# Hybrid RG-LRU / retention / expert-choice MoE step on one core: the recurrence's gates moved one chunk earlier, its chain cut by direction, and the final norm done tile by tile

## What is computed

```python
h = rms_norm(x) * (1 + sc1) + sh1                   # sc, sh, g: from ada_w and the condition
xl, yl, q, k, v, g = split(h @ w_in)                # six blocks of 512 columns
xl = depthwise_conv4(xl)
r, gi = sigmoid(xl @ wa[d] + ba[d]), sigmoid(xl @ wi[d] + bi[d])      # d = forward, backward
log_a = -8 * r * softplus(-lam);  a = exp(log_a)
u = sqrt(-expm1(2 * log_a)) * gi * xl
h_t = a_t * h_(t-1) + u_t                           # scanned in both directions, then summed
lru_out = (hf + hb) * gelu(yl)
ret_out = rms(retention(rope(q), rope(k), v)) * silu(g)
x1 = x + g1 * rms_norm(concat(lru_out, ret_out) @ w_out)
h2 = rms_norm(x1) * (1 + sc2) + sh2
f = 16 experts, each takes its top tokens (64 latent, 16 context): silu(h2 wg) * (h2 wu) @ wd, added up
y = x1 + g2 * rms_norm(f)
```

## Time and profile before

| | us |
|---|---|
| median of 3 runs | 1654.58 (1652.83 to 1656.48) |
| the profiled execution, its own time | 1652.98 |
| its span, first to last instruction | 1651.2 |
| PE busy | 1516.5 (92% of the span) |
| DVE busy | 1282.8 (78%) |
| ACT busy | 1008.4 (61%) |
| POOL busy | 194.0 (12%) |
| mean granted clock of PE, of 1 | 0.949 |

### The profile page before, as it was taken

The page is one execution under the profiler, slowest core; times in us unless marked ns, Lnnn a source line. Parts: engine busy times, 40 slices in busy tenths (PEclk is TensorE's granted clock), DMA queues, the critical chain, the costliest instruction groups (busy, mean ns, idle before and its releaser), DMA issues.

```text
span 1651.2 us, 19540 instructions
## 1 busy us (share of the span) xinstructions
PE 1516.5 (92%) x7022; PEld 1052.7 (64%) x7022; DVE 1282.8 (78%) x1127; ACT 1008.4 (61%) x807; POOL 194.0 (12%) x110
## 2 busy tenths in 40 slices
PE   5799898879948999999999999999999999999991
PEld 2698776547745666666666666666666666666650
DVE  5647736784557988989889898898988989889873
ACT  6313444242325777777777777777777777777752
POOL 0301210000000020220202202022020220201200
PEclk9899899999858999999999999999999999999995
DMA  9421123357138999999999999999999999999943
GB/s 354 125 77 52 51 77 97 100 199 296 41 101 307 364 371 379 390 359 381 376 375 376 364 384 372 373 387 359 385 373 367 386 366 382 369 375 369 367 186 135
DMA packets 127667, 476.71 MB, mean 289 GB/s; under 512 B 11406, under 2 KB 21898, under 8 KB 111244
## 3 DMA queue, kind: packets, MB, share of 16 engines
q1 hardware_dynamic: 116304, 447.77, 72.7%
q0 software_dynamic: 3728, 13.11, 3.1%
q10 hardware_dynamic: 7596, 15.30, 2.6%
HBM read 462.51 MB, written 13.64 MB: 288 GB/s over the span
## 4 chain that ended last, share of the span: by engine, by line
PE 83%; DVE 8%; ACT 3%; DMA 3%; issue 2%; POOL 0%; SPq 0%; ACTq 0%; POOLq 0%; DVEq 0%
PE banks L965 22%; PE banks L969 22%; PE banks L966 22%; PE banks L329 3%; PE banks L330 3%; PE banks L331 3%; PE banks L986 2%; DVE w_lo L295 1%; ACT w_hi L291 1%; DMA raw<-in_ada_w 1%; PE banks L919 1%; PE banks L758 1%; PE banks L836 1%; PE banks L955 1%; DVE arena L1184 1%
## 5 line engine op out<-in xcount | busy, mean ns | idle before, releaser
L295 DVE TENSOR_TENSOR w_lo<-raw,w_hi 128x2048 fp32r<-128x2048 f32 x232 | 531.1, 2290 | 174.0 <-ACT w_hi L291 169.7
L291 ACT CAST w_hi<-raw 128x2048 fp32r<-128x2048 f32 x232 | 443.1, 1912 | 134.7 <-PE banks L969 66.5
L965 PE MATMUL banks<-w_hi,act_lo 128*80 128x512 f32 x1152 | 457.5, 397 | 1.7 <-DVE act_lo L1414 1.7
L966 PE MATMUL banks<-w_hi,act_hi 128*80 128x512 f32 x1152 | 454.9, 395 | 0.0
L969 PE MATMUL banks<-w_lo,act_hi 128*80 128x512 f32 x1152 | 314.6, 395 | 0.0
L295 DVE TENSOR_TENSOR w_lo<-arena,w_hi 128x2048 fp32r<-128x2048 f32 x96 | 220.0, 2291 | 37.7 <-ACT w_hi L291 37.7
L965 PEld LDWEIGHTS banks<-w_hi,act_lo 128*80 128x80 f32 x1152 | 173.2, 150 | 95.6 <-issue 2.6
L969 PEld LDWEIGHTS banks<-w_lo,act_hi 128*80 128x80 f32 x1152 | 171.0, 148 | 96.7 <-issue 1.4
L966 PEld LDWEIGHTS banks<-w_hi,act_hi 128*80 128x80 f32 x1152 | 171.7, 149 | 92.4 <-issue 1.6
L291 ACT CAST w_hi<-arena 128x2048 fp32r<-128x2048 f32 x96 | 183.6, 1913 | 62.4 <-PE banks L969 62.4
L295 DVE TENSOR_TENSOR act_lo<-raw,act_hi 128x2048 fp32r<-128x2048 f32 x64 | 146.7, 2292 | 17.3 <-ACT act_hi L291 17.3
(11 more groups left out here) (225 smaller groups left out, 1764.7 us busy)
## 6 DMA issues: line engine op xcount, KB each, us to landing
raw<-in_exp_down SPq DMA_DIRECT2D x126, 1024.0 KB, 7.0
raw<-in_exp_gate SPq DMA_DIRECT2D x66, 1024.0 KB, 7.6
arena<-in_exp_up SPq DMA_DIRECT2D x64, 1024.0 KB, 7.6
raw<-in_exp_up SPq DMA_DIRECT2D x64, 1024.0 KB, 8.0
arena<-in_exp_gate SPq DMA_DIRECT2D x62, 1024.0 KB, 7.4
raw<-in_ada_w SPq DMA_DIRECT2D x24, 1024.0 KB, 5.6
raw<-in_w_in SPq DMA_DIRECT2D x12, 1024.0 KB, 5.2
arena<-in_x_lat ACTq DMA_DIRECT2D x8, 512.0 KB, 10.4
```

The lines of the kernel that those rows point to most:

```text
L291: nc.scalar.copy(w_chunk(w_hi, n), raw_chunk(n)).then_inc(hi_done, 1)
L295: nc.vector.tensor_tensor(w_chunk(w_lo, n), raw_chunk(n), w_chunk(w_hi, n), ALU.subtract).then_inc(lo_done, 1)
L965: mm(dst, x[j][1], wh[:, j, at], start=(first and j == 0), stop=False)
L966: mm(dst, x[j][0], wh[:, j, at], start=False, stop=False)
```

## The change

Four edits. (1) Chunk `ct` of the recurrence moves from the first half of block `2 + ct` to the second half of block `1 + ct`. In blocks xl, q and k its four PE steps stand inside and behind the last unit (after k = 1, 3, 5 and 7); in block v behind tiles 0 to 3 of the second half. ACT does all of the chunk, exp, tanh and roots too, before it splits the next weight chunk; in block v it copies tiles of v between the gates. DVE's parts move to the first half of the next block, and the `split_lo` of the half before stands behind `lru_scan`. (2) POOL's product, DVE's square, weighting and product, and ACT's root are cut by direction, each with its own count. (3) ACT issues the retention loads of heads 0 and 1 before the second last split of block g, not after g's tiles. (4) At the end POOL copies the last column of indices before it waits for expert 15's rows; ACT takes a root ahead, which loads that table early; DVE multiplies each tile with the gain before its root is known, and then does one fused operation; squares, roots and sums run tile by tile; SP issues the stores.

```diff
-GATES_AT = {0: 0, 2: 1, 4: 2, 6: 3}
+    g_times = raw[:, 0:3, :].rearrange("p r (t d) -> p (r t) d", t=2)
...
 # SP, behind the loads of the five tiles
+        for t in range(TILES):
+            sync.wait_ge(fin_y, t + 1)
+            sync.dma_start(y_lat[t * P:(t + 1) * P, :] if t < 4 else y_ctx, facc[:, t, :]).then_inc(out_y, 16)
...
 # ACT
         def lru_sqrt(ct):
-            act.wait_ge(lr_w, ct + 1)
-            nc.scalar.activation(lr_t[:, :, :], lr_t[:, :, :], ACT.Sqrt).then_inc(lr_sq, 1)
+            for d in range(2):
+                act.wait_ge(lr_w, 2 * ct + d + 1)
+                nc.scalar.activation(lr_t[:, d, :], lr_t[:, d, :], ACT.Sqrt).then_inc(lr_sq, 1)
...
         for m in range(N_WIN, N_MID):
             bi, half = (m - N_WIN) // 2, m % 2
-            ct = GATES_AT.get(m - N_WIN - 4)
+            ct = bi - 1 if half and 1 <= bi <= CT else None
             if ct is not None:
-                for s in range(4 * ct, 4 * ct + 4):
-                    lru_gates_out(s)
-
+                for j in range(4):
+                    lru_gates_out(4 * ct + j)
+                    if bi == 4:
+                        tok_out(0, j)
+                if bi == 4:
+                    tok_out(0, TILES - 1)
+                lru_exp(ct)
+                lru_sqrt(ct)
             if bi == 0:
                 yl_out(2 * half)
-            if half and bi >= 4:
-                for t in range(TILES - 1):
-                    tok_out(bi - 4, t)
             if half and bi == 5:
-                tok_out(1, TILES - 1)
+                for t in range(TILES):
+                    tok_out(1, t)
+            if bi == 5 and not half:
                 ret_loads(0)
                 ret_loads(1)
             split_hi(act, m + WS)
...
-            if half and bi == 4:
-                tok_out(0, TILES - 1)
-            if ct is not None:
-                lru_exp(ct)
-                lru_sqrt(ct)
...
-        for t in range(TILES):
-            act.wait_ge(f_in[t], 16)
+        nc.scalar.activation(sm[:, S_X1:S_X1 + 8], sm[:, S_X1:S_X1 + 8], ACT.Sqrt).then_inc(root_warm, 1)
+        for t in range(TILES + 1):
+            if t < TILES:
+                act.wait_ge(f_in[t], 16)
+                if t == 0:
+                    act.wait_ge(x1_sq, TILES)
+                nc.scalar.activation(xn2[:, t, :], facc[:, t, :], ACT.Square, accum_out=sm[:, S_FIN + t:S_FIN + t + 1]).then_inc(fin_sq, 1)
             if t:
...
-            nc.scalar.activation(xn2[:, 0, :], facc[:, t, :], ACT.Square, accum_out=sm[:, S_FIN + t:S_FIN + t + 1]).then_inc(fin_sq, 1)
-        root(S_O)
-        for t in range(TILES):
-            act.wait_ge(fin_y, t + 1)
-            act.dma_start(y_lat[t * P:(t + 1) * P, :] if t < 4 else y_ctx, facc[:, t, :]).then_inc(out_y, 16)
+                root(S_O + t - 1, 1)
...
 # PE, blocks yl to k, then v and g
-                    if n - N_WIN - 4 in GATES_AT and k == 3:
-                        lru_gates(4 * GATES_AT[n - N_WIN - 4] + 2 * (u % 2))
+                    if bi and u == 3 and k in (1, 3, 5):
+                        lru_gates(4 * (bi - 1) + k // 2)
                 last.then_inc(w_used if u % 2 else win_ps, 1)
-                if n - N_WIN - 4 in GATES_AT:
-                    lru_gates(4 * GATES_AT[n - N_WIN - 4] + 2 * (u % 2) + 1)
+                if bi and u == 3:
+                    lru_gates(4 * (bi - 1) + 3)
...
-                if n - N_WIN - 4 in GATES_AT and u < 4:
-                    lru_gates(4 * GATES_AT[n - N_WIN - 4] + u)
+                if half and bi == 4 and u < 4:
+                    lru_gates(4 * (bi - 1) + u)
...
 # DVE
         def lru_weight(ct):
-            dve.wait_ge(lr_exp, 4 * (ct + 1))
-            step(tt(lr_r, lr_a, lr_a, ALU.mult))
-            stt(lr_t, lr_r, 1.0, lr_t, ALU.add, ALU.mult).then_inc(lr_w, 1)
+            for d in range(2):
+                dve.wait_ge(lr_exp, 4 * ct + 2 * (d + 1))
+                step(tt(lr_r[:, d, :], lr_a[:, d, :], lr_a[:, d, :], ALU.mult))
+                stt(lr_t[:, d, :], lr_r[:, d, :], 1.0, lr_t[:, d, :], ALU.add, ALU.mult).then_inc(lr_w, 1)
...
-            dve.wait_ge(lr_sq, ct + 1)
-            dve.wait_ge(lr_gx, ct + 1)
-            step(tt(lr_t, lr_t, lr_g, ALU.mult))
             for d, h0 in ((0, par[:, R_H0 + ct:R_H0 + ct + 1]), (1, par[:, R_H0 + 4 + ct:R_H0 + 5 + ct])):
+                dve.wait_ge(lr_sq, 2 * ct + d + 1)
+                dve.wait_ge(lr_gx, 2 * ct + d + 1)
+                step(tt(lr_t[:, d, :], lr_t[:, d, :], lr_g[:, d, :], ALU.mult))
...
+            ct = bi - 2 if bi >= 2 and not half else None
+            if ct is not None:
+                lru_weight(ct)
+                lru_scan(ct)
+                split_lo(dve, m - 1 + WS)
+            for side in range(2):
+                if bi == 1:
+                    conv_unit(2 * half + side)
+                if bi in (2, 3):
+                    rope_terms(bi - 2, (qT, kT)[bi - 2], 2 * half + side)
+                if side == 0 and ct is not None:
+                    lru_out(ct)
+                if side == 0 and not (half and 1 <= bi <= CT):
+                    split_lo(dve, m + WS)
...
-        dve.wait_ge(fin_sq, TILES)
-        rstd(sm[:, S_O:S_O + TILES], sm[:, S_FIN:S_FIN + TILES], D)
         dve.wait_ge(gr_ev, 8)
-        for t in range(TILES):
-            step(stt(facc[:, t, :], facc[:, t, :], sm[:, S_O + t:S_O + t + 1], g_row[:, t // 4, :], ALU.mult, ALU.mult))
-            tt(facc[:, t, :], facc[:, t, :], x1[:, t, :], ALU.add).then_inc(fin_y, 1)
+        last_roots = []
+        for t in range(TILES + 1):
+            if t < TILES:
+                dve.wait_ge(f_in[t], 16)
+                tt(g_times[:, t, :], facc[:, t, :], g_row[:, t // 4, :], ALU.mult).then_inc(fin_g, 1)
+                dve.wait_ge(fin_sq, t + 1)
+                rstd_start(sm[:, S_O + t:S_O + t + 1], sm[:, S_FIN + t:S_FIN + t + 1], D)
+                last_roots.append(roots[0])
+            if t:
+                dve.wait_ge(root_out, last_roots[t - 1])
+                dve.wait_ge(fin_g, t)
+                stt(facc[:, t - 1, :], g_times[:, t - 1, :], sm[:, S_O + t - 1:S_O + t], x1[:, t - 1, :], ALU.mult, ALU.add).then_inc(fin_y, 1)
...
 # POOL
+            for h in range(2 * half, 2 * half + 2):
+                if half and h == 3 and 1 <= bi <= CT:
+                    for d in range(2):
+                        pool.wait_ge(gt_ev, 8 * (bi - 1) + 4 * (d + 1))
+                        nc.gpsimd.tensor_tensor(lr_g[:, d, :], lr_g[:, d, :], xc[:, bi - 1, :], ALU.mult).then_inc(lr_gx, 1)
...
             pool.wait_ge(sl_ct, 1)
-            pool.wait_ge(ye_rd, 2 * e + 2)
+            if last:
+                pool.wait_ge(f_add, 16 * e + 16)
+            else:
+                pool.wait_ge(ye_rd, 2 * e + 2)
             nc.gpsimd.tensor_copy(slot_out[:, :], slots[:, bass.ds(e, 1)]).then_inc(sc_ct, 2)
             pool.wait_ge(sl_ct, 1)
             pool.wait_ge(sc_ct, 2 * e + 2)
+            if last:
+                pool.wait_ge(ye_rd, 2 * e + 2)
```

More of the change, by code:

```diff
@@ L201, in build @@
     root_in, root_out = sem("root_argument"), sem("root_taken")
-    fin_sq, fin_y = sem("f_squares"), sem("y_ready")
+    fin_sq, fin_g, fin_y, root_warm = map(sem, ("f_squares", "f_times_gain", "y_ready", "root_table"))
     aw = ada_w.rearrange("(k p) n -> p k n", p=P)
@@ L462, in tok_out @@
                 if t == 0:
-                    act.wait_ge(lr_gx, CT)
+                    act.wait_ge(lr_gx, 2 * CT)
                 nc.scalar.activation(sg[:, t, :], bank[:, :], ACT.Silu).then_inc(g_ev, 1)
@@ L664, in _ @@
         body(LAST, 1, True)
-        for t in range(TILES):
-            act.wait_ge(f_in[t], 16)
-            if t:
-                act.wait_ge(fin_sq, t)
-            else:
-                act.wait_ge(x1_sq, TILES)
-            nc.scalar.activation(xn2[:, 0, :], facc[:, t, :], ACT.Square, accum_out=sm[:, S_FIN + t:S_FIN + t + 1]).then_inc(fin_sq, 1)
-        root(S_O)
-        for t in range(TILES):
-            act.wait_ge(fin_y, t + 1)
-            act.dma_start(y_lat[t * P:(t + 1) * P, :] if t < 4 else y_ctx, facc[:, t, :]).then_inc(out_y, 16)
+        nc.scalar.activation(sm[:, S_X1:S_X1 + 8], sm[:, S_X1:S_X1 + 8], ACT.Sqrt).then_inc(root_warm, 1)
[5 more added lines that the diff above has]
+                nc.scalar.activation(xn2[:, t, :], facc[:, t, :], ACT.Square, accum_out=sm[:, S_FIN + t:S_FIN + t + 1]).then_inc(fin_sq, 1)
+            if t:
+                root(S_O + t - 1, 1)
     @block.tensor
@@ L1206, in _ @@
             bi, half = (m - N_WIN) // 2, m % 2
-            parts = (lru_weight, lru_scan, lru_out) if half and bi >= 2 else ()
-            if bi == 1:
-                conv_unit(2 * half)
-            for part in parts[:2]:
-                part(bi - 2)
-            if bi in (2, 3):
-                rope_terms(bi - 2, (qT, kT)[bi - 2], 2 * half)
-            for part in parts[2:]:
-                part(bi - 2)
-            split_lo(dve, m + WS)
-            if bi == 1:
```

(18 more changed lines are left out.)

## The result

The changed kernel takes 1628.06 us (median of 4 runs, 1623.88 to 1629.64) where the one before took 1655.37 (4 runs): a ratio of 0.9833, interval 0.9811 to 0.9855. That is 27.3 us faster, where the prediction had 28.8 us and a time of 1626 us. Its own profiled execution took 1627.80 us with a span of 1626.0; the one before took 1652.98 with 1651.2 (all groups of rows come from it). Between these two profiles it is 25.2 us.

The account below looks back on a forecast made before the run. PE bounds the experts, untouched here; gains lie before and behind. 14.9 + 7.2 + 6.7 = 28.8 us off the profiled 1652.98 gave 1624.2, adjusted to the median 1625.8, stated as 1626 us; range 1621 to 1634 us.

Parts of the forecast that it names:

- The stage of `w_in`: From first gate step to first score product: two PE stalls and the slow clock behind them go, 14.9 us won.
- Condition (a): Gate steps in xl, q and k, 1.76 us apart: ACT's read fits in 1.4 us, so PE never waits.
- Condition (b): `lr_done` precedes the next chunk's gates: chunk 2's at 206.4, allowed until 208.3, about 2 us to spare.
- rival of a chain too long: Recurrence: late `lr_done` of chunk 2 stalls PE at chunk 3's second gate step; 20.8 us won, 1634 us; chance 0.14.
- Condition (c): Deferred `split_lo`s in the `w_in` stage come before their weight chunks are wanted, with 18 us to spare.
- From block g to the value products: First score product to value products: 8.5 us instead of 15.7, loads hidden; 7.2 us won (5.2 to 7.6).
- rival of the clock: PE's wait before the third score product lowers its clock through the value products: 5 us lost, 1631 us; chance 0.13.
- my list of steps: First score product to value products: silu, splits, masks, score products and context part, together 8.5 us.
- The scatter: Kernel's end: taking POOL's index copy and its start out of the way wins 0.3 us (0.2 to 1.0).
- The final norm: Last five tiles, DVE-bound at 2.85 us each, ending at 1641.3 for 1648.05: 6.7 us won, scatter's 0.3 included.
- Behind the retention, nothing: Later stages, fed by their own rings and predecessors, only move forward as they are: no further gain.
- The slower rival: ACT reads over 1.76 us hold PE's clock low through xl, q, k and v: 51 us lost, 1675 us; chance 0.04.

Follow-up runs that it names:

- gates_together: The changed kernel with the four gate steps of chunks 0 to 2 back to back instead of 12 matmuls apart: 1643.46 us, ratio 0.9937.
- uncut: The changed kernel with square, weighting, product and root of both directions in one instruction again: 1627.69 us, ratio 0.9838.
- rec_only: The kernel before with gates one chunk sooner, cut by direction and earlier retention loads, without the scatter's and norm's part: 1635.76 us, ratio 0.9878.
- stores_act: The changed kernel with the five result stores issued by ACT behind its last root, not by SP: 1630.06 us, ratio 0.9854.
- no_warm: The changed kernel without the root that loads the table ahead of the final norm: 1625.16 us, ratio 0.9823.
- after_again: The changed kernel, unaltered, measured again on the chip of its two halves: 1627.29 us, ratio 0.9821.
- masks_first: The changed kernel with DVE's split of the last weight chunk moved behind head 0's masks: 1622.33 us, ratio 0.9796.
- tail_only: The kernel before with the scatter's and the final norm's part of the change alone: 1648.05 us, ratio 0.9945.
- cut_only: The kernel before with the cut by direction alone, the gates left where they were: 1650.2 us, ratio 0.9971.
- late_loads: The changed kernel with the retention loads issued behind the silus of block g again: 1629.8 us, ratio 0.9849.

## Why the prediction was right

*The stage of `w_in`, 14.9 us.* Predicted 249.0 for the first score product, measured 248.88; no wait of PE in it. Condition (a): the reads take 1.26 us, and the distance of 1.76 us holds them. `gates_together` shows what it protects: 14.2 us in the trace, 16 in the median. Condition (b): `lr_done` of chunk 2 predicted at 206.4, measured 206.2 (205.35 + 0.82). I took 2 us for the cut, measured 2.1. I had also written that without the cut nothing would be left of the slack; `uncut` has just that, and PE doesn't wait. The rival of a chain too long falls. Condition (c) shows no wait either.

*From block g to the value products, 7.2 us.* The step that was off: 8.5 us from the first score product to the value products. The changed kernel's profile has 10.39 us, for 15.51 before in the same view, so 5.1 us were won, a little under the lower bound of 5.2. Two things lie in it. In four profiles of the same schedule where the clock stayed full (`rec_only`, `stores_act`, `no_warm`, `uncut`) it is 8.85 us, so my list of steps was 0.35 us short: the third score product starts 5.56 us behind the first where the list has 5.38, and from there to the value products it is 3.29 us where it has 3.12. The rest, 1.5 us, is the clock: behind the same 1.96 us of waiting the third and fourth score products take 1.98 us in those four profiles, 3.52 in the changed kernel's and 2.94 in `after_again`'s. That was the rival of the clock, priced at 5 us because I carried it on into the value products. Their lines take 3.74 us in all these profiles, so the lower level ended ahead of them and cost 1 to 1.5. I had this rival at 0.13; it came, at a third of its price or less.

*The order of releasers* was as laid out: first the chain, then the loads, then DVE's split. `masks_first` shows the last of these: 5.0 us in the median, of which 2.2 are the wait itself and 1 to 1.5 the clock behind it; the rest is not larger than what executions differ by.

*The scatter, 0.3 us.* From the start of ACT's last pair at L660 to the scatter 2.43 us became 2.12: 0.3 us. The copy of the indices now stands ahead of the wait, and the scatter still starts 0.86 us behind ACT's end (1599.92 to 1600.78), much as the first gather did behind its indices. No run has this edit alone.

*The final norm, 6.4 us.* Measured 7.55. The mis-sized term is the tile's period: 2.85 us predicted (its three parts add to 2.88), 2.6 measured (1612.49, 1615.09, 1617.68). I gave the two small operations 0.4 us with their waits; in the chain they take 0.17 with their issue times (0.07 + 0.02 + 0.04 + 0.04), and the plain operation 1.14 where I had 1.2, since the first small one starts inside its last tenth. Over the whole stretch it is 13.16/5 = 2.63 us a tile: 5 x 0.22 = 1.1 us, the difference. The stores' 0 to 0.5 us was right for the way they are issued: from the last store's issue to the end of the span it is 3.2 us, before 3.1. What it would cost to leave them with ACT I had not asked.

*Behind the retention, nothing.* Right as far as the runs can tell, but not between the two profiles. From the value products to the first gather it is 210.9 us for 209.4 before. In the ten experiments this stretch took 208.1 to 214.5 us: 213.2 and 212.9 in `tail_only` and `cut_only`, whose schedule there is that of before, and 208.1 in `gates_together`. It doesn't go with the schedule, and the profile of before had a short one. That is what makes the profiled 25.2 us less than the 27.3 to 28.7 of the medians, as far as can be told. A part of it is the gates' rows: 4.0 us before and 6.5, 5.5, 5.9, 7.1, 5.8, 6.4, 5.9, 3.7, 6.1, 5.8 and 4.1 in the changed kernel and the ten experiments (in the order `after_again`, `rec_only`, `tail_only`, `masks_first`, `uncut`, `late_loads`, `gates_together`, `cut_only`, `stores_act`, `no_warm`), behind a wait for DVE of 1.2 to 2.4 us. The same eight matmuls take up to twice their time, as at the lower level of PE's clock, whose mean is 0.87 from 340 to 380 us in the changed kernel's profile. What sets it from one execution to the next stays open. The experts' stretch from first gather to scatter is 1130.6 us for 1129.9, 1.0 longer with the scatter's 0.3 counted; the ten experiments, the changed kernel again among them, have 1129.0 to 1130.0, so the change didn't do that.

*The slower rival* (gates that starve PE's clock, 1675 us) was tested by its own condition, though not at its own places: in `gates_together` ACT's reads are longer than the distance. It costs 14 to 16 us, not 51; in its profile the clock stayed at 1.00 in the stretches around the first two chunks and fell around the third (0.83 from 190 to 200 us, 1.00 again behind it). Pauses of 0.7 to 1.4 us did not hold PE at its lower level through a unit there.

*The sum.* In the profiles 14.9 + 5.1 + 0.3 + 7.55 us were won, 27.9 for the 28.8 of the sum. That this is so near is partly luck: the stretch behind block g gave 2.1 us less than forecast and the final norm 1.15 more.

## What to carry to other kernels

Lay out the stage by its work at full speed first: the gap to the measured stage is what the stalls and the slow clock behind them cost together, and here it was 14.9 us, what removing them gave. Then ask at each removed stall who is late next and try the one-line move for that as well: here the split of a weight chunk that nobody wanted yet stood in front of the masks, and moving it was worth 2.2 us of waiting and the slow clock behind it, 5 us in the medians. When a step moves onto an engine's program, look at what else that engine issues: in `stores_act` stores that left together landed later (4.9 us) than stores that left one by one (2.7), and in `late_loads` four loads issued ahead of a split made everything behind it 1.5 us late.

## What the hardware showed that I had not expected

PE's clock behind the same wait differs from execution to execution. Behind 1.96 us of waiting for the same mask, the same two score products took 1.98 to 3.6 us in seven profiles, and the gates' rows 3.7 to 7.1 us in twelve, there behind waits of 1.2 to 2.4 us. From the value products to the first gather the twelve profiles lie between 208.1 and 214.5 us. A single profile can be 3 to 6 us off by this; a change worth 3 us has to be read in its own stretch, and in medians of more than four executions.

DVE and POOL hold each other up. In `cut_only`, DVE's timeline and POOL's at chunk 0:

```profile
147.51 1.82 DVE L1185 TENSOR_TENSOR arena<-arena 128x640 f32<-128x640 f32 x1
149.37 2.08 DVE L1186 SCALAR_TENSOR_TENSOR arena<-arena 128x640 f32<-128x640 f32 x1
151.37 2.19 DVE L1185 TENSOR_TENSOR arena<-arena 128x640 f32<-128x640 f32 x1
153.60 0.83 DVE L1186 SCALAR_TENSOR_TENSOR arena<-arena 128x640 f32<-128x640 f32 x1
```

```profile
148.61 4.28 POOL L1504 TENSOR_TENSOR arena<-arena 128x640 f32<-128x640 f32 x2
```

A half instruction takes DVE 0.83 us alone and 1.8 to 2.2 beside POOL's products; POOL's two halves take 4.28 us, and 1.56 each in the changed kernel, where no such DVE instruction runs beside them. The Trainium skill, "SBUF — State Buffer", SBUF: two separate sides, has the two engines share a port pair that one instruction holds to its end while the other is blocked, and says so for DVE operations with two SBUF inputs. The rows agree: here 1.0 to 1.4 us are added to a DVE instruction, a little under one half product of POOL.

Before, this stood in the chains of chunks 0 and 1, ahead of both stalls of PE: DVE's weighting took 6.6 us there (2.48 and 4.13) and 3.0 at chunks 2 and 3 (1.49 twice), where POOL was done. In the changed kernel the products are over before DVE's weighting starts at every chunk (at chunk 2 at 192.45 and 193.70), and in `uncut` too, where its two instructions take 1.49 us each. So the new order also took this collision, 3.6 us, off the chain; the prediction named it only as a danger to the new chain.
